# Conditioning weights loaded by halves of the channels, two blocks at once on four column groups, and a reordered rate stage, in a one-core decoder block

## The chip, the cores and the metric

The program runs on one core of a Trainium2 chip. The metric is the device time of one execution, in microseconds (us), taken as the median of several runs. Everything is computed in 32-bit floats; large products are made as three products of a high and a low part.

## The reference, cut to what matters

The kernel computes one decoder block for 1024 tokens of width 1024: adaLN conditioning, a mixing layer (RWKV-7 and latent attention side by side), and a mixture of 32 experts. The change touches how the block begins and how the rates of the RWKV branch are prepared.

```python
mod = jax.nn.silu(c) @ w_ada[l] + b_ada[l]            # (1, 6 * 1024)
sh_m, sc_m, gt_m, sh_f, sc_f, gt_f = jnp.split(mod, 6, axis=-1)
h = modulate(rmsnorm(x, g_norm_mix[l]), sh_m, sc_m)   # y * (1 + sc) + sh
z = h @ w_in[l]
...
w_log = -jax.nn.softplus(-(w0 + jnp.tanh(zw) @ w_decay_up)) - 0.5
decay = jnp.exp(-jnp.exp(w_log.astype(jnp.float32)))
a = jax.nn.sigmoid(a0 + za @ w_a_up)
kk = heads(zk * k_k).astype(jnp.float32)
kk = kk / jnp.maximum(jnp.sqrt(jnp.sum(kk * kk, axis=-1, keepdims=True)), 1e-12)
k = zk * (1 + (a - 1) * k_a)
```

So no product with `w_in` can be made before the shift and scale of its channels are known: 2048 columns of `w_ada` (8.4 MB), and the root mean square of each token row.

## The kernel before, in words

Each engine has its own hand-written stream of instructions; streams meet only at semaphores. SP issues nearly all transfers, in order, on one queue. The program is cut into blocks with a barrier between them; four stages matter here.

**Opening.** SP (line 421 on) asks for `c`, the whole table of constants (`cst`, 680 KB), seven of the eight 128-row tiles of `x` (512 KB each), biases and gains repeated over partitions, then eight pieces of `w_ada` of 1024 KB (one for each of eight interleaved groups of input channels `k`, all 2048 output columns; `Rows.load`, line 320). The eighth tile of `x` takes the place of the first in `xt` and is asked for only after that one has been transposed. ACT squares and sums each row tile (L543) and takes roots of four tiles at a time (L548); DVE scales the rows (L687); PE transposes them (L860) into three pairs of PSUM banks; ACT and DVE each copy one bank of a pair out (L552, L692) to `xn`, whose partitions are channels. In between, PE makes the conditioning products (`Rows.products`, L332): the vector silu(c), repeated over 32 columns as `crep`, is the stationary operand, and four blocks of 512 output columns go to the four column groups of the array, so that one PSUM bank holds shift and scale on four groups of 32 partitions. After the last piece DVE adds the bias (L339), makes (1 + scale) x gain (L709), PE turns the four blocks of rows to columns (L889), and DVE copies them to `mcol` (L712).

**Column tiles.** For each of eight channel groups `k`, ACT writes the high part of the modulated channels (`hh`, L572), DVE the exact value (L720) and the low part (`hl`, L351). PE then makes for `k` the products with the first two column tiles of `w_in` (24 matmuls of 512 columns, L355 to L357), whose own high and low parts are `wr_h` and `wr_l`. After all eight, PE goes on to the eight token tiles of the latent projections (`mla`, 24 matmuls of 416 columns each) and to the other column tiles, with the latent attention's preparation between them.

**Rates.** The next block, from 311 us: ACT squares the keys (L1022), PE sums them by head (L1099), ACT takes a root (L1025), DVE inverts it (L1054), PE spreads it back over the channels (`norms_back`, L1091). For each of four channel tiles PE makes two up-projections (decay and in-context rate, L1076), ACT two sigmoids and a scaled copy (L1029, L1032, L1037), DVE three products (L1058, L1063, L1064). The second row of conditioning (`rows2`: eight pieces of 1024 KB, L332) is loaded and multiplied in the same block; its buffer has room for six pieces.

**Scan.** The block after that starts with four prefix scans on DVE (L1451), their exponents (L1456, L1459) and exponentials on ACT (L1324 on), while POOL makes `rk` (L1245), clears `S` and builds four tiles `headrk` (L1293).

## Time and profile before

| | us |
|---|---|
| median of 3 runs (lowest, highest) | 1516.15 (1515.04, 1517.63) |
| the profiled execution's own time | 1512.1 |
| its span, first to last instruction | 1510.3 |
| PE busy in the span | 1381.2 (91%) |
| DVE busy | 761.9 (50%) |
| ACT busy | 492.7 (33%) |
| POOL busy | 317.5 (21%) |
| mean granted TensorE clock, share of 2.4 GHz | 0.961 |

A line of a timeline reads: start in the span, length, engine, line of the kernel, operation, output<-input, shapes, count; in brackets the time for which the engine stood idle before it and what ended that. A matmul of 32-bit floats shows as more than one record. PE is matmul time, PEld the loading of the stationary operand, which goes on beside it. "DMA packets" lines give what all queues moved in a stretch.

### The profile page before, as it was taken

Reading aid. Unit: us, or ns where it says so; the run is one execution under the profiler, and the core shown is the slowest. Engines: PE = TensorE matmul, PEld = TensorE weight load, DVE = VectorE, ACT = ScalarE, POOL = GpSimd, SP = SyncE. Lnnn points to the kernel's source line nnn. Section 1 sums busy time; section 2 is a strip of 40 time slices with the busy share of each in tenths; the row PEclk is TensorE's granted clock in tenths of the full one; section 3 lists DMA queues with packets and bytes.
Section 4 is the critical chain, followed back from the end, with each engine's and each line's share of the span. In section 5 each row is a group of like instructions: output and inputs, shape, how many; then the busy total and the mean of one; then the engine's idle time right before and its main releaser. Section 6 shows DMA issues by size and latency. Waiting matters only on the chain. (4 is left out here: it accounts for less than half of the span.)

```text
span 1510.3 us, 32868 instructions
## 1 busy us (share of the span) xinstructions
PE 1381.2 (91%) x14305; PEld 996.3 (66%) x14305; DVE 761.9 (50%) x1134; ACT 492.7 (33%) x891; POOL 317.5 (21%) x332
## 2 busy tenths in 40 slices
PE   4899999986999998899989999999996799999995
PEld 3587777745999998677767888787885333333332
DVE  3815676756677666544548455656455422111111
ACT  4433233263344443544445444313111111111110
POOL 0002121206556542011110000000000123333323
PEclk8999999997999999899999999999997699999998
DMA  9761322270000001750003113514227999999992
GB/s 372 278 187 51 91 75 66 75 268 2 4 4 4 4 11 41 207 202 15 15 27 141 56 56 112 195 53 161 84 84 274 358 354 392 382 403 380 394 370 59
DMA packets 74956, 238.20 MB, mean 158 GB/s; under 512 B 12216, under 2 KB 37304, under 8 KB 58048
## 3 DMA queue, kind: packets, MB, share of 16 engines
q1 hardware_dynamic: 63872, 219.31, 38.9%
q0 software_dynamic: 10944, 16.82, 4.6%
q8 instruction: 112, 1.84, 0.5%
q14 instruction: 28, 0.23, 0.0%
HBM read 207.74 MB, written 51.40 MB: 172 GB/s over the span
## 5 line engine op out<-in xcount | busy, mean ns | idle before, releaser
L3052 PE MATMUL ps<-gu,xT 128*32 128x512 f32 x1296 | 177.0, 605 | 4.9 <-DMA gu<-w_e_up 4.2
L3268 DVE TENSOR_TENSOR sg<-sg,ps 128x256 f32<-128x256 f32 x25 | 10.5, 421 | 205.4 <-ACT sg L3138 205.4
L3052 PEld LDWEIGHTS ps<-gu,xT 128*32 128x32 f32 x1296 | 46.8, 111 | 98.0 <-issue 94.4
L2939 POOL DMA_INDIRECT out<-YTM,home x48 | 75.2, 1566 | 168.2 <-DVE YTM L3277 160.9
L355 PE MATMUL ps<-hh,wr_h 128*128 128x512 f32 x224 | 93.5, 417 | 4.5 <-DVE hl L351 3.8
L357 PE MATMUL ps<-hh,wr_l 128*128 128x512 f32 x224 | 88.9, 397 | 0.0
L356 PE MATMUL ps<-hl,wr_h 128*128 128x512 f32 x224 | 88.9, 397 | 0.0
L3070 PE MATMUL ps<-dn,hidT 128*32 128x512 f32 x648 | 86.7, 592 | 0.5 <-ACT hidT L3142 0.5
L2119 DVE TENSOR_REDUCE nmax<-ps 128x1 f32<-128x896 f32 (+4 forms) x64 | 45.8, 752 | 71.4 <-PE ps L2017 70.9
L2957 POOL MEMSET xg<- 128x3072 f32 x1 | 2.7, 2658 | 366.1 <-PE ps L2444 366.1
L1287 POOL TENSOR_TENSOR off<-mats,cst 128x256 f32<-128x256 f32 x80 | 67.4, 861 | 48.0 <-PE ps L1709 47.7
L1502 DVE TENSOR_TENSOR inverses<-inverses,ps 128x512 f32<-128x512 f32 (+1 forms) x80 | 49.9, 630 | 50.8 <-PE ps L1725 50.4
L516 POOL TENSOR_TENSOR qk<-qk,g_row 128x768 f32<-128x768 f32 x16 | 37.9, 2390 | 173.3 <-DVE qk L792 173.3
L1725 PE MATMUL ps<-inverses,xx 64*64 64x64 f32 x1280 | 70.8, 218 | 0.0
L2012 PE MATMUL ps<-kT,qT 96*128 96x512 f32 (+3 forms) x160 | 64.8, 514 | 3.1 <-ACT causalr L2100 3.1
L3142 ACT ACTIVATE hidT<-ps 128x256 f32<-128x256 f32 x25 | 9.6, 384 | 166.5 <-PE ps L3039 166.5
L1722 PE MATMUL ps<-xx,inverses 64*64 64x64 f32 x1024 | 62.8, 220 | 0.2 <-issue 0.2
L1725 PEld LDWEIGHTS ps<-inverses,xx 64*64 64x64 f32 x1280 | 62.9, 135 | 0.1
L355 PE MATMUL ps<-hs,M 128*128 128x512 f32 x144 | 57.6, 400 | 1.6 <-DVE hs L351 1.6
L3052 PE MATMUL ps<-gu_last,xT 128*32 128x512 f32 x240 | 57.8, 594 | 0.0
L3070 PEld LDWEIGHTS ps<-dn,hidT 128*32 128x32 f32 x648 | 24.1, 110 | 50.3 <-issue 49.7
L356 PE MATMUL ps<-hs,M 128*128 128x512 f32 x144 | 56.1, 389 | 0.0
(440 smaller groups left out, 3433.3 us busy)
## 6 DMA issues: line engine op xcount, KB each, us to landing
gu<-w_e_gate SPq DMA_DIRECT2D x29, 1024.0 KB, 17.5
gu<-w_e_up SPq DMA_DIRECT2D x29, 1024.0 KB, 23.4
dn<-w_e_down SPq DMA_DIRECT2D x29, 1024.0 KB, 16.9
wbuf<-w_ada SPq DMA_DIRECT2D x16, 1024.0 KB, 12.8
wbuf<-w_ada SPq DMA_DIRECT2D x16, 512.0 KB, 4.6
wraws<-w_gates SPq DMA_DIRECT2D x16, 512.0 KB, 4.9
wr<-w_rwkv SPq DMA_DIRECT2D x14, 512.0 KB, 3.6
qk_cols<-YTM SPq DMA_DIRECT2D x8, 768.0 KB, 5.5
```

The lines of the kernel that those rows point to most:

```text
L355: nc.tensor.matmul(out, wt[0], mov[0], start=(k == 0), stop=False)
L356: nc.tensor.matmul(out, wt[0], mov[1], start=False, stop=False)
L357: return nc.tensor.matmul(out, wt[1], mov[0], start=False, stop=(k == kn - 1))
L1287: nc.gpsimd.tensor_tensor(off[:, g], mats[:, n % 2, 4 * g:4 * g + 4, 0], cst[:, a:a + CHUNK].unsqueeze(1).broadcast_to([P, 4, CHUNK]), ALU ...
L1502: nc.vector.tensor_tensor(now, now, add, ALU.add).then_inc(sm["t_ev"], 1)
L1722: nc.tensor.matmul(o[rows, 0:CHUNK], tt(j)[rows, hh, 1], xx[rows, hh], start=True, stop=True)
L1725: m = nc.tensor.matmul(o[rows, CHUNK:], xx[rows, hh], tt(j)[rows, hh, 1], start=True, stop=True)
L2012: nc.tensor.matmul(ps[:, 2 * (u % 2) + at // 512, at % 512:at % 512 + to - at], q, kT_[:, at - o * P:to - o * P], start=True, stop=True)
L2119: nc.vector.tensor_reduce(nmax[:, n:n + 1], score(u, i, o), AX.X, ALU.max, negate=True)\
L2939: pool.indirect_dma_start(out=out[0], out_offset=bass.IndirectOffsetOnAxis(ap=col.bitcast(u32), axis=0), in_=yo[:, buf], in_offset=None, b ...
L3052: last = nc.tensor.matmul(ps[part, GB[b]], xT[:, b, k, part], gu[expert(m, c_) % WB][:, :, k], start=(k == 0), stop=(k == KD - 1))
L3070: last = nc.tensor.matmul(ps[part, 6 + half], hidT[:, b, k, part], dn[expert(m, c_) % WB][:, k, half * 512:(half + 1) * 512], start=(k == ...
```

## The change

**Opening.** A new class `HalfRows` takes the place of `Rows` for the first 2048 conditioning columns. It loads sixteen pieces of 512 KB: for half `h` of the channels and input group `k`, 512 columns of shift and 512 of scale. First all eight pieces of half 0, then two column tiles of `w_in`, then half 1. One call of `products` takes two input groups `k` at once, each with two blocks, on the four column groups, and the bank then holds two partial sums of each, which are added after the transposition. Biases and gains come as 24 short rows that PE transposes to columns at the start. Only the 128-column identity of the constants is loaded early (behind two tiles of `x`), the rest after all transposes. The eighth tile of `x` has a place of its own (in `zm`), DVE squares tiles 1 and 3, and roots are taken two tiles at a time. PE begins with channel 0 when half 0 is modulated, with products of half 1 between channels 0, 1 and 2.

```diff
+            def load(self, sp, h, k):
+                src = w_ada_v[:, k, 0:2 * D].rearrange("p (a h n) -> p a h n", a=2, h=2)[:, :, h]
+                sp.dma_start(self.piece(h, k), src).then_inc(self.w_in[h][k // 2], 16)
+
+            def products(self, pe, h, pair):
+                if h == 0 and pair == 0:
+                    pe.wait_ge(self.rep_s, 1)
+                pe.wait_ge(self.w_in[h][pair], 32)
+                for i in range(2):
+                    for a in range(2):
+                        m = nc.tensor.matmul(ps[QUARTERS[2 * i + a], self.banks[h]], self.crep[:, 2 * pair + i],
+                                             self.piece(h, 2 * pair + i)[:, a], start=(pair == 0), stop=(pair == CT - 1))
+                m.then_inc(self.mm, 1)
+
+            def to_row(self, dve, h):
+                dve.wait_ge(self.mm, CT * (h + 1))
+                nc.vector.tensor_copy(self.row[:], ps[:, self.banks[h]]).then_inc(self.done, 1)
...
-                    sp.dma_start(cst[:], consts).then_inc(const_in, 16)
-                    for t in range(XT):
+                    for t in range(NT):
                         load_x(t)
+                        if t == 1:
+                            sp.dma_start(cst[:, 0:P], consts[:, 0:P]).then_inc(const_in, 16)
+                            rows0.load_bias(sp)
                     for k in range(KD):
-                        rows0.load(sp, k)
...
+                        rows0.load(sp, 0, k)
+                    for c_ in range(2):
+                        load_weights(c_)
+                    for k in range(KD):
+                        rows0.load(sp, 1, k)
                     sp.dma_start(wm[:], w_mla).then_inc(wm_in, 16)
+                    sp.wait_ge(tr, 2 * NT)
+                    sp.dma_start(cst[:, P:], consts[:, P:]).then_inc(const_in, 16)
...
+                    def columns(h):
+                        col = mcol[:, :, h]
+                        dve.wait_ge(mcol_mm, h + 2)
+                        sums_ = ps[:, 7].rearrange("p (j b a n) -> p b a j n", j=CT, b=2, a=2)[:, :, :, :, 0]
+                        nc.vector.tensor_tensor(col, sums_[:, 0], bg[:, 0:2, h], ALU.add).then_inc(mcol_s, 1)
+                        dve.wait_ge(mcol_s, 3 * h + 1)
+                        nc.vector.tensor_tensor(col, col, sums_[:, 1], ALU.add).then_inc(mcol_s, 1)
+                        dve.wait_ge(mcol_s, 3 * h + 2)
+                        nc.vector.tensor_tensor(col[:, 1], col[:, 1], bg[:, 2, h], ALU.mult).then_inc(mcol_s, 1)
...
+                    rows0.to_row(dve, 0)
+                    dve.wait_ge(bg_s, 2)
+                    columns(0)
+                    weights(0, 1)
...
+                    modulated(0)
+                    weights(1, 2)
+                    for k in range(1, CT):
+                        modulated(k)
+                    nc.vector.memset(zT[:, 0:2, 0:1], 0.0).then_inc(zero, 1)
+                    rows0.to_row(dve, 1)
+                    columns(1)
+                    dve.wait_ge(const_in, 32)
+                    dve.wait_ge(mcol_s, 6)
+                    for k in range(CT, KD):
+                        modulated(k)
```

**PE at the opening.** In the order of PE's instructions `cst,xt` and `cst,zm` are the transposes of `x`, `wbuf,crep` the conditioning products, `cst,arows` the turning of rows into columns. Before:

```order
L860 MATMUL ps<-cst,xt 128x128 x32
L332 MATMUL ps<-wbuf,crep 32x512 x8
L860 MATMUL ps<-cst,xt 128x128 x24
L332 MATMUL ps<-wbuf,crep 32x512 x16
L860 MATMUL ps<-cst,xt 128x128 x8
L332 MATMUL ps<-wbuf,crep 32x512 x8
L889 MATMUL ps<-cst,arows 128x128 x4
L355 MATMUL ps<-hh,wr_h 128x512
```

Now:

```order
L998 MATMUL ps<-cst,arows 128x24
L959 MATMUL ps<-cst,xt 128x128 x48
L380 MATMUL ps<-wbuf,crep 32x512 x4
L959 MATMUL ps<-cst,xt 128x128 x8
L380 MATMUL ps<-wbuf,crep 32x512 x4
L959 MATMUL ps<-cst,zm 128x128 x8
L380 MATMUL ps<-wbuf,crep 32x512 x8
L982 MATMUL ps<-cst,arows 128x128 x4
```

Sixteen of 32 conditioning products stand ahead of the first channel, the other sixteen between the first three channels (eight after channel 0, eight after channel 1).

**SP at the opening.** `xt` and `zm` are the tiles of `x`, `wbuf` the conditioning weights, `wr` and `wm` those of the first products. Now:

```order
L481 DMA ccol<-c 128x8
L477 DMA xt<-x 128x1024 x2
L485 DMA cst<-consts 128x128
L367 DMA arows<-b_ada 16x128
L368 DMA arows<-g_norm_mix 8x128
L477 DMA xt<-x 128x1024 x5
L477 DMA zm<-x 128x1024
L372 DMA wbuf<-w_ada 128x2x512 x8
L480 DMA wr<-w_rwkv 128x1024 x2
L372 DMA wbuf<-w_ada 128x2x512 x8
L493 DMA wm<-w_mla 128x3328
L495 DMA cst<-consts 128x1232
```

Before, the constants stood second, and all eight pieces of 1024 KB were asked for ahead of the rest.

**Rates.** The selection matrix `sel` and the first two of the eight pieces of `rows2` are loaded in the block before (the buffer now has five places, one of them laid so that it is free early); up-projections are made rate by rate, not half by half of the tokens, so that the decay's sigmoid can start after two products; the first products of `rows2` stand between the sums by head.

```diff
-                        for n in range(2):
-                            for j, (w, src, done) in enumerate(((wup[0:64], Z(WA)[0:64], dec),
-                                                                (wup[64:128], Z(WA)[64:128], a_done))):
-                                if c_ and n == 0:
-                                    pe.wait_ge(done, c_)
+                        for j, (w, src, done) in enumerate(((wup[0:64], Z(WA)[0:64], dec),
+                                                            (wup[64:128], Z(WA)[64:128], a_done))):
+                            if c_:
+                                pe.wait_ge(done, c_)
+                            for n in range(2):
                                 m = nc.tensor.matmul(ps[:, 6 * j + n], w[:, c_ * P:(c_ + 1) * P],
                                                      src[:, n * 512:(n + 1) * 512], start=True, stop=True)
-                                if n:
-                                    m.then_inc(up_mm, 1)
+                            m.then_inc(up_mm, 1)
```

**PE in the block of the rates.** `zT,YTM` are up-projections, `sq,norm_sel` sums by head, `rn,norm_sel` norms spread back, `wbuf,crep` products of `rows2`. Before:

```order
L1076 MATMUL ps<-zT,YTM 128x512 x4
L1099 MATMUL ps<-sq,norm_sel 32x256 x16
L1091 MATMUL ps<-rn,norm_sel 128x256 x4
L332 MATMUL ps<-wbuf,crep 32x512 x4
L1076 MATMUL ps<-zT,YTM 128x512 x4
L1091 MATMUL ps<-rn,norm_sel 128x256 x4
L332 MATMUL ps<-wbuf,crep 32x512 x4
```

Now:

```order
L1190 MATMUL ps<-zT,YTM 128x512 x4
L1211 MATMUL ps<-sq,norm_sel 32x256 x8
L339 MATMUL ps<-wbuf,crep 32x512 x4
L1211 MATMUL ps<-sq,norm_sel 32x256 x8
L339 MATMUL ps<-wbuf,crep 32x512 x8
L1204 MATMUL ps<-rn,norm_sel 128x256 x4
L339 MATMUL ps<-wbuf,crep 32x512 x4
L1190 MATMUL ps<-zT,YTM 128x512 x4
L1204 MATMUL ps<-rn,norm_sel 128x256 x4
L1190 MATMUL ps<-zT,YTM 128x512 x4
```

Four of the eight products of `rows2` now come before the second up-projection, and none between the later channel tiles.

**Scan.** POOL waits for the four scans of the first period before it starts, and the four `headrk` tiles are built by DVE behind its first exponents.

```diff
+                    wait("cum", 0, CT)
                     prepare(0)
                     nc.gpsimd.memset(S[:], 0.0).then_inc(init, 1)
-                    for c_ in range(CT):
-                        nc.gpsimd.tensor_scalar(headrk[:, c_], C("heads"), PC("r_k", c_), None, ALU.mult)\
-                          .then_inc(init, 1)
...
+                    for c_ in range(CT):
+                        nc.vector.tensor_scalar(headrk[:, c_], C("heads"), PC("r_k", c_), None, ALU.mult)\
+                          .then_inc(init, 1)
```

## Rows read from the trace of the kernel before

**Rows 1.** The page's first line: span of the profiled execution.
```profile
span 1510.3 us, 32868 instructions
```
**Rows 2.** DMA answer, stretches 7 to 12, 36 to 41 and 41 to 48 us.
```profile
DMA packets 571, 2.08 MB, mean 415 GB/s; under 512 B 64, under 2 KB 64, under 8 KB 571
...
DMA packets 260, 2.16 MB, mean 432 GB/s; under 512 B 31, under 2 KB 31, under 8 KB 31
...
DMA packets 1206, 2.21 MB, mean 316 GB/s; under 512 B 128, under 2 KB 940, under 8 KB 1132
```
**Rows 3.** Timeline of the opening, 6 to 32 us: row tiles of x.
```profile
6.95 1.06 ACT L543 ACTIVATE tmp<-xt 128x1024 f32<-128x1024 f32 x1 [4.21 <-DMA xt<-x]
...
13.71 2.74 DVE L687 TENSOR_SCALAR xt<-xt,rs 128x1024 f32<-128x1024 f32 x4
...
16.51 0.33 SPq L428 DMA_DIRECT2D xt<-x  x1
16.52 0.69 DVE L692 COPY xn_late<-ps 128x512 f32<-128x512 f32 x1
...
27.90 1.06 ACT L543 ACTIVATE tmp<-xt 128x1024 f32<-128x1024 f32 x1 [7.21 <-DMA xt<-x]
...
30.55 5.38 PE L860 MATMUL ps<-cst,xt 128*128 128x128 f32 x24 [7.81 <-DVE xt L687]
```
**Rows 4.** Timeline, 35 to 51 us: from the last conditioning weights to the first product.
```profile
35.86 3.82 PE L332 MATMUL ps<-wbuf,crep 128*32 128x512 f32 x32
...
41.79 0.16 PEld L332 LDWEIGHTS ps<-wbuf,crep 128*32 128x32 f32 x8 [1.00 <-DMA wbuf<-w_ada]
...
44.16 0.68 DVE L339 TENSOR_TENSOR arows<-arows,ps 128x512 f32<-128x512 f32 x1
...
45.62 0.66 PE L889 MATMUL ps<-cst,arows 128*128 128x128 f32 x4 [2.77 <-DVE arows L709]
46.32 0.17 DVE L712 COPY mcol<-ps 128x16 f32<-128x16 f32 x1 [0.75 <-PE ps L889]
...
46.53 1.24 ACT L572 ACTIVATE hh<-YTM,mcol 128x1024 fp32r<-128x1024 f32 x1 [3.74 <-DVE mcol L712]
...
47.90 0.81 DVE L720 TENSOR_SCALAR YTM<-YTM,mcol 128x1024 f32<-128x1024 f32 x1 [1.41 <-ACT hh L572]
...
48.75 1.23 DVE L351 TENSOR_TENSOR hl<-YTM,hh 128x1024 fp32r<-128x1024 f32 x1
...
50.12 0.77 PE L355 MATMUL ps<-hh,wr_h 128*128 128x512 f32 x1 [3.84 <-DVE hl L351]
```
**Rows 5.** Windows: length, busy PE, PEld, DVE, ACT, POOL, clock, DMA share, GB/s.
```profile
50.00:53.00 3.00, 2.88 (x7) 2.33 (x8) 2.93 (x4) 3.00 (x4) 0.00 (x0) 0.50 1.06 370
53.00:76.00 23.00, 23.00 (x102) 18.84 (x101) 21.25 (x34) 7.63 (x6) 1.39 (x1) 0.99 0.58 225
```
**Rows 6.** Timeline at 74 us: the first latent product.
```profile
74.06 0.35 PE L355 MATMUL ps<-wm_h,hh 128*128 128x416 f32 x1
```
**Rows 7.** The loads of column tiles (L431), 512 KB each: least, median, most.
```profile
DMA to landing us min/median/max: 3.2/3.6/17.1
```
**Rows 8.** Timeline of the rates, 312 to 343 us.
```profile
312.54 1.99 PE L1076 MATMUL ps<-zT,YTM 64*128 64x512 f32 x8 [1.74 <-DMA norm_sel<-norm_sel]
...
319.50 2.45 PE L1091 MATMUL ps<-rn,norm_sel 32*128 32x256 f32 x8 [3.10 <-DVE rn L1054]
...
323.74 3.29 PE L1076 MATMUL ps<-zT,YTM 64*128 64x512 f32 x8
...
327.07 1.11 ACT L1029 ACTIVATE lw<-ps,pc 128x1024 f32<-128x1024 f32 x1 [5.13 <-PE ps L1076]
...
337.00 4.50 PE L332 MATMUL ps<-wbuf,crep 128*32 128x512 f32 x40
```
**Rows 9.** Timeline of the scan's start, 342 to 358 us.
```profile
342.88 2.53 DVE L1451 TENSOR_TENSOR_SCAN cum<-cst,lw 128x128 f32<-128x128 f32 x4 [0.55 <-PEq L1004]
...
355.74 1.37 DVE L1451 TENSOR_TENSOR_SCAN cum<-cst,lw 128x128 f32<-128x128 f32 x4 [2.18 <-PE ps L1629]
```

More of the change, by code:

```diff
@@ L208, in build @@
         mod_out = ctx.enter_context(nc.semaphore("mod_out"))
[L209 removed]
+        up_in, sel_in = (ctx.enter_context(nc.semaphore(n)) for n in ("up_in", "sel_in"))
+        first_rows = [ctx.enter_context(nc.semaphore(f"first_rows{i}")) for i in range(2)]
         y_out4 = ctx.enter_context(nc.semaphore("y_out4"))
@@ L309, in __init__, with place @@
                 self.b_in, self.mm, self.done = sems(st, f"ab_in{col}", f"amm{col}", f"adone{col}")
-                self.w_in = slots(st, f"aw_in{col}", self.room)
+                self.w_in = list(first) + slots(st, f"aw_in{col}", self.room - len(first))
+                self.order = order or list(range(self.room))
+            def place(self, i):
+                return self.wbuf[:, self.order[i % self.room]]
             def cols(self, j):
@@ L900, in _ @@
                                 m.then_inc(z_mm, 1)
+                    pe.wait_ge(const_in, 16)
+                    pe.wait_ge(rows0.b_in, 32)
+                    nc.tensor.transpose(ps[:, 7, 0:24], small0[0:24], C("ident")[0:24, 0:24]).then_inc(mcol_mm, 1)
+                    for t in range(NT):
+                        row_transposes(t)
+                        if t >= NT - 3:
+                            for pair in range(t - NT + 3, t - NT + 4 if t < NT - 1 else CT):
+                                rows0.products(pe, 0, pair)
+                    row_columns(0)
+                    channel(0)
+                    for pair in range(2):
+                        rows0.products(pe, 1, pair)
+                    channel(1)
+                    for pair in range(2, CT):
+                        rows0.products(pe, 1, pair)
+                    channel(2)
+                    row_columns(1)
+                    for k in range(3, KD):
+                        channel(k)
                     def half_column(c_, n):
@@ L1006, in _ @@
                 def _(sp):
-                    for k in range(CT):
+                    for k in range(2, CT):
                         rows2.load(sp, k)
```

242 lines of the change are left out of this document (138 added, 104 removed).

## The prediction

> **What bounds the kernel now.** I read the page first, then windows and the timeline of the two stages that the change touches. PE is busy for 91% of the span, so over most of the kernel a change elsewhere is worth nothing. The exceptions are stretches in which PE has no work yet, and there each microsecond counts, because the later stages start on events of the earlier ones: whatever comes off the front shifts all that follows. The span is 1510.3 us [rows 1], the profiled execution's own time 1512.1, the median 1516.15; I make the sum against the execution and lay the difference on the median, which is 4.05 above it.
>
> **The opening** is bound by transfers. The last piece of the conditioning weights lands at 41.79 and the first real product starts at 50.12 [rows 4]. Up to then the queue has moved 0.70 MB of constants, 4.19 of `x`, 8.39 of `w_ada`, 1.05 of `wr` and some biases, 14.7 MB in about 39.5 us, without a pause. The rate depends on the packet: 415 GB/s with packets of 4 KB, 432 with 8 KB and more, 316 where most are of 1 KB [rows 2]. A second delay hides in it: the eighth tile of `x` is asked for at 16.51, behind four pieces of 1 MB, and its squares start at 27.90, with ACT idle for 7.21 us, and PE for 7.81 until its transposes at 30.55 [rows 3]. From the last piece to the first product runs a chain with no slack: product, bias, gain, turning, copy, high part, exact value, low part, 41.79 to 50.12, so 8.3 us [rows 4]. After that PE is full: 3 us at a clock of 0.50 (the 1.2 GHz level, after PE had been nearly idle), then 0.99 (2.4 GHz) with 23.00 of 23 us busy [rows 5]. The first latent product starts at 74.06 [rows 6], 23.9 us after the first channel.
>
> **The rates**, from 311 to 342 us, are a chain over PE, ACT and DVE. PE waits 1.74 for `norm_sel`, later 3.10 for the inverse norms, and ACT waits 5.13 for the second up-projection [rows 8]. PE ends the block with five products, 337.00 to 341.5.
>
> **Part 1, up to the first product: 15.3 us less.** When does half 0 land? `x` starts at about 2.2 us and takes 4.19/0.415 = 10.1. Half 0 is 4.19 MB in packets of 2 KB. No row shows that size; between 316 and 415 GB/s [rows 2] I take 365, since packets of 4 KB run close to those of 8 and only those of 1 KB fall off: 11.5 us. With 1.5 us for the landing itself (0.70 MB of constants and a first tile of 0.52 take 2.9 at that rate from 2.2, and its squares start at 6.95 [rows 3]), half 0 has landed at 25.3, the pair of `wr` at 27.8, and half 1 (another 11.5) at 39.3.
>
> Row preparation is no longer hidden and decides. DVE starts on it at about 8 (identity and short biases stand behind two tiles of `x`). It has two squarings (two-input, as L351, 1.23 [rows 4]; I take 1.3), eight scalings (2.74 for four [rows 3]) and eight copies of 0.69 [rows 3], and four round trips for roots at about 0.9: 2.6 + 5.5 + 5.5 + 3.6 = 17.2, so 25.2. Laid out tile by tile with the waits for PE (5.38 for three tiles [rows 3], so 1.8 a tile, and the last tile is scaled at 24.2), the last copy ends at 27.7. The last two pairs of products follow PE's last transposes: a pair is as much work as one piece before, 3.82/4 = 0.95 [rows 4], so about 29.0. Then the copy to a row 0.69, turning 0.66, three small operations at 0.2 in place of one of 0.17 (the wide gain operation goes), high part 1.2, exact value 0.81, low part 1.23, handovers 0.5 [rows 4]: 5.7. The weights' low part lies beside the high part on ACT. First product at 34.8 in place of 50.12. Bounds: 32, where half 0's landing and the same chain alone count; 38.5, where each of the last four tiles costs another microsecond of waiting between ACT, DVE and PE.
>
> **Part 2, channels: 5.1 us given back.** What came before the channels partly moves into them: four pairs of products for half 1, 3.8 (3.5 without the last one's tail), the second turning, 0.5. PE reaches it at 34.8 + 13.7 = 48.5. DVE and ACT then need three small operations, high part, exact value and low part, 3.9, under channel 3, which takes 23.0/8 = 2.9 [rows 5]: PE waits about 1.1. Behind DVE's wait for the constants stand all four late channels, but these land at 39.3 + 1.70/0.43 + 0.63/0.4 = 45, and the wait is reached at 49. Half 1 is needed at 34.8 + 8.7 = 43.5, 4 us after it lands. Channels take 29.0 in place of 23.9. Bounds: 3.8 with no wait, 8 if half 1 or the constants are late. The latent stage thus starts 10.2 us earlier. SP's queue: rows4, gains and the spill of `h` stand behind the same bytes as before and end at about 66; DVE asks for them at 61, but its work there is wanted by PE only some 20 us later. I cost that at nothing.
>
> **Part 3, rates: 5.0 us less.** The first up-projection no longer waits 1.74, but the root behind it is held by ACT's squares and its table load, so that is worth 0. After 319.50 eight products of `rows2` lay on PE's path (three between, five at the end, 4.50/5 = 0.9 each), now five: 2.7. The 3.10 us gap before 319.50 is filled with two products, so the clock should stay up, and the first spreading (2.45) and the second up-projection (3.29) each get back up to half: 2.9 at most, of which I take 2.3. The order rate by rate starts ACT's sigmoid half a projection (1.0) earlier, but PE's own 3.3 a round then decides. Bounds 2.7 and 6.5. The two early pieces cost the block before nothing: PE is full there and the queue is not.
>
> **Part 4, scan: 1.2 us less.** The first four scans take 2.53 beside POOL, the next four 1.37 without [rows 9]. POOL now waits for them, and 2.53 - 1.37 = 1.16. Four small operations move to DVE, hidden while ACT makes the exponentials; if not, they cost 0.7. Bounds 0 and 2.5.
>
> **Sum.** 15.3 - 5.1 + 5.0 + 1.2 = 16.4 us off: 1512.1 - 16.4 = 1495.7 for such an execution, and **1499.7** for the median. That the products share four column groups adds nothing: four were in use before, and as many matmuls remain.
>
> A rule that speaks against the change: the halves make sixteen transfers of 512 KB of eight of 1024. What the trace shows: eight transfers of 512 KB behind each other ran at 415 GB/s [rows 2], 1.26 us each, while one of that size alone takes 3.2 from issue to landing [rows 7], about 2 more. The Trainium skill (DMA: Bandwidth & Descriptors, Bandwidth) says to batch transfers to 1 MiB or more to get three quarters of the peak, and gives 341 GB/s for a single one of 1 MB. By that rule the fixed part would be paid for each half piece, and the sum would become the last rival's below; by the row the pieces overlap, and the sum stands.
>
> **Rivals.**
> - **Row preparation is slower than laid out** (0.17). For: DVE, ACT and PE hand each tile round, and ACT has its squares between copies. Against: bare work sums to 25. First product at 39: 1499.7 + 4.2 = 1503.9.
> - **Only the front gains** (0.07): the rates stay bound by PE at the low clock or by ACT. 1499.7 + 5.0 = 1504.7.
> - **It all comes out better** (0.11): first product at 32, no wait inside the channels, 6.5 from the rates: 1499.7 - 2.8 - 1.1 - 1.5 = 1494.3.
> - **The shift is swallowed later** (0.03), at a transfer that does not start on an event: no change, 1516. Against: I found none; SP's waits at the experts are on PE and DVE.
> - **Slower: transfers of half size pay their fixed part one by one** (0.02). At 2 us each [rows 2, 7], sixteen land half 1 31 us later, at 70. From its landing to the latent stage run one pair 0.95, the chain of 5.2 and four channels, 11.2: 17.4 us. The stage would start at 87.7 instead of 74.06, and with 6.2 from the other parts the time is 1516.15 + 13.6 - 6.2 = 1523.5. It decides from a landing at 63 on. Against stands the row of 415 GB/s.
>
> **How the numbers follow.** The forecast has 0.60. Its own bounds, not all at one end, give 1495 to 1504. The range takes in the first three rivals as well: 1494 to 1507, which leaves out less than 2 in 10. Faster by over 0.2% (3 us, about what a measurement of this kernel can tell from no change): 0.95. Within: 0.03. Slower: 0.02.
>
> **What would show it.** The first product of 128x512 with `wr_h` at 34.8 (32 to 38.5); DVE's last copy at 27.7, after half 0's landing at 25.3; the first latent product at 63.8 with a gap of PE near 1 us behind channel 3; the block of the rates 5 us shorter, with ACT's second sigmoid waiting well under 5 us; the first four scans near 1.4. I am wrong if half 1 or the constants hold DVE, if the clock stays at 1.2 GHz beyond some 3 us of channel 0, or if the rates end within 2 us of before.

## The result, and the profile after

| | before | changed |
|---|---|---|
| median (lowest, highest), us | 1516.89 (1515.04, 1518.90) | 1503.57 (1501.70, 1504.10) |
| runs | 4 | 4 |
| profiled execution's own time | 1512.1 | 1503.23 |
| its span | 1510.3 | 1501.4 |
| PE busy in the span | 1381.2 (91%) | 1380.9 (92%) |
| mean granted clock | 0.961 | 0.965 |

The ratio is 0.9919, 95% interval 0.9900 to 0.9938: 13.3 us faster between the medians, where 16.4 were forecast. The interval runs from 9.4 to 15.2 us, so the forecast saving lies just outside it. The two profiled executions differ by only 8.9: single executions scatter by several us, and the last experiments measure by how much.

The opening of the changed kernel, as a timeline (start, length, engine, line, operation), 19 to 35 us. These rows answer to [rows 3] and [rows 4]:

```profile
24.43 0.69 DVE L760 COPY xn_late<-ps 128x512 f32<-128x512 f32 x1 [1.33 <-PE ps L959]
...
25.88 1.07 PE L380 MATMUL ps<-wbuf,crep 128*32 128x512 f32 x8 [0.49 <-DMA wbuf<-w_ada]
27.01 0.69 DVE L386 COPY arows<-ps 128x512 f32<-128x512 f32 x1 [1.89 <-PE ps L380]
27.14 1.06 ACT L389 ACTIVATE wr_h<-wr 128x1024 fp32r<-128x1024 f32 x1 [2.55 <-DMA wr<-w_rwkv]
...
28.92 0.16 DVE L777 TENSOR_TENSOR mcol<-mcol,arows 128x4 f32<-128x4 f32 x1
...
29.31 1.06 ACT L389 ACTIVATE wr_h<-wr 128x1024 fp32r<-128x1024 f32 x1 [1.11 <-DMA wr<-w_rwkv]
30.27 4.62 ACT L634 ACTIVATE hh<-YTM,mcol 128x1024 fp32r<-128x1024 f32 x4
...
31.63 0.81 DVE L782 TENSOR_SCALAR YTM<-YTM,mcol 128x1024 f32<-128x1024 f32 x1 [1.42 <-ACT hh L634]
32.48 1.23 DVE L392 TENSOR_TENSOR hl<-YTM,hh 128x1024 fp32r<-128x1024 f32 x1
...
33.76 0.79 PE L396 MATMUL ps<-hh,wr_h 128*128 128x512 f32 x1 [5.34 <-DVE hl L392]
```

Three things are to be seen. The last copy of the rows (L760) ends at 25.12, and only then, at 25.88, do the last two pieces of half 0 let PE go on: the landing of half 0 ends last, not the row preparation. The columns are ready at 29.08, but ACT waits 1.11 us for the second weights (`wr`, which stand behind half 0 on the queue), makes their high part first and gets to `hh` at 30.27. The first product starts at 33.76.

The same timeline from 44 to 53 us, the turning of half 1 and the gap behind the fourth channel. The kernel before has nothing in this place:

```profile
44.87 0.69 DVE L386 COPY arows<-ps 128x512 f32<-128x512 f32 x1 [4.06 <-PE ps L380]
...
47.62 0.60 PE L982 MATMUL ps<-cst,arows 128*128 128x128 f32 x4
48.26 0.17 DVE L773 TENSOR_TENSOR mcol<-ps,arows 128x8 f32<-128x8 f32 x1 [2.70 <-PE ps L982]
...
52.36 0.50 PE L396 MATMUL ps<-hh,wr_h 128*128 128x512 f32 x1 [1.34 <-DVE hl L392]
```

The rows of half 1 are out of PSUM at 45.56 and wait two microseconds for PE, which turns them only behind the third channel, at 47.62. From there to the low part runs the same chain as for half 0, and PE stands for 1.34.

Windows of the changed kernel (length, busy time of PE, PEld, DVE, ACT, POOL, clock, DMA share, GB/s) answer to [rows 5]:

```profile
33.80:36.70 2.90, 2.90 (x7) 2.32 (x8) 2.87 (x3) 1.09 (x1) 0.00 (x0) 0.51 1.04 386
36.70:50.00 13.30, 13.30 (x75) 8.17 (x75) 5.23 (x10) 1.14 (x1) 0.00 (x0) 1.00 1.05 350
50.00:63.60 13.60, 12.26 (x53) 9.65 (x52) 11.43 (x9) 7.41 (x6) 1.60 (x1) 1.00 1.04 403
```

And the DMA answer for 15.0 to 25.5 us, while half 0 lands, answers to [rows 2]:

```profile
DMA packets 2036, 4.09 MB, mean 390 GB/s; under 512 B 126, under 2 KB 126, under 8 KB 2036
```

The low clock takes 2.9 us of the first channel, about as before the change, and packets of 2 KB run at 390 GB/s.

The rates, which answer to [rows 8]:

```profile
307.91 1.06 PE L339 MATMUL ps<-wbuf,crep 128*32 128x512 f32 x8 [1.24 <-DMA wbuf<-w_ada]
...
308.98 1.47 PE L1204 MATMUL ps<-rn,norm_sel 32*128 32x256 f32 x8
...
311.05 1.06 PE L339 MATMUL ps<-wbuf,crep 128*32 128x512 f32 x8 [0.60 <-DMA wbuf<-w_ada]
...
312.05 2.00 PE L1190 MATMUL ps<-zT,YTM 64*128 64x512 f32 x8
...
314.07 1.11 ACT L1143 ACTIVATE lw<-ps,pc 128x1024 f32<-128x1024 f32 x1 [2.55 <-PE ps L1190]
...
322.88 3.64 PE L339 MATMUL ps<-wbuf,crep 128*32 128x512 f32 x32
323.43 1.28 DVE L1172 SCALAR_TENSOR_TENSOR kk<-zT,pc,ps 128x1024 f32<-128x1024 f32 x1
...
326.14 1.22 DVE L1178 TENSOR_TENSOR aa<-aa,kk 128x1024 f32<-128x1024 f32 x1
```

The spreading (2.45 before) and the second up-projection (3.29 before) run at the full clock. ACT waits 2.55 us for the second up-projection, where it waited 5.13 before. The last four products of `rows2` end at 326.5, while DVE is still at its three products: no longer PE but DVE ends the block. And two products of `rows2` wait for their weights, 1.24 and 0.60 us. Only the second of these waits holds the up-projection: during the first PE had to wait for the inverse norms anyway, which DVE has ready at 308.92.

The scan's start, which answers to [rows 9]:

```profile
328.51 1.37 DVE L1572 TENSOR_TENSOR_SCAN cum<-cst,lw 128x128 f32<-128x128 f32 x4 [0.55 <-PEq L1118]
329.92 0.69 DVE L1577 TENSOR_TENSOR ex<-cum,lw 128x512 f32<-128x512 f32 x1
329.96 1.77 POOL L1368 TENSOR_TENSOR rk<-zT 128x512 f32<-128x512 f32 x1 [28.58 <-DVE cum L1572]
330.53 1.75 DVE L1580 TENSOR_TENSOR ex<-cum 128x512 f32<-128x512 f32 x1
...
332.32 1.06 ACT L1445 ACTIVATE ex<-ex 128x1024 f32<-128x1024 f32 x1 [2.56 <-DVE ex L1580]
...
338.31 0.68 DVE L1605 TENSOR_TENSOR zT<-zT,ps 128x512 f32<-128x512 f32 x1
...
339.14 1.09 PE L1753 MATMUL ps<-cst,ce 128*128 128x128 f32 x4 [3.01 <-DVE zT L1605]
```

The scans take 1.37, as forecast, but POOL now runs beside the second exponent, which takes 1.75; the kernel before makes it in 0.68 (there it is L1459, started at 346.18). The last two lines are the end of the chain to the first pair: DVE's last multiplication (L1605), and behind it PE's transposes of `ce` and `ex`, here at the lower clock (1.09 and 1.06). In the kernel before, with its scan's start at 342.88, the same multiplication stood here:

```profile
352.89 0.67 DVE L1484 TENSOR_TENSOR zT<-zT,ps 128x512 f32<-128x512 f32 x1
```

So it starts 10.01 us behind the scan's start before, and 9.80 after the change.

Starts in the span of each execution, read off the timelines (the two first columns are the two kernels of the table above, "again" is a second execution of each):

| | before | changed | before again | changed again |
|---|---|---|---|---|
| first product | 50.1 | 33.8 | 50.1 | 33.5 |
| first latent product | 74.1 | 63.6 | 73.9 | 63.5 |
| rates | 311.3 | 300.9 | 311.2 | 300.7 |
| scan | 342.9 | 328.5 | 342.8 | 328.8 |
| first pair of the scan | 356.4 | 341.9 | 356.3 | 341.3 |
| attention | 621.8 | 610.2 | 623.3 | 611.7 |
| experts | 1190.4 | 1180.0 | 1193.3 | 1180.5 |
| end | 1510.3 | 1501.4 | 1516.1 | 1501.0 |

### The profile page after: what moved, and what is told of

Same layout as the page of the kernel before. It is cut to its first block and busy times, and to the rows that moved or that the text cites. A ratio compares the mean times of both kernels' runs of the same rounds, so it can differ in the third digit from the quotient of the medians.

```text
span 1501.4 us, 32904 instructions
## 1 busy us (share of the span) xinstructions
PE 1380.9 (92%) x14310; PEld 996.1 (66%) x14310; DVE 762.7 (51%) x1153; ACT 490.3 (33%) x890; POOL 314.7 (21%) x328
## 5 line engine op out<-in xcount | busy, mean ns | idle before, releaser
L396 PE MATMUL ps<-hs,M 128*128 128x512 f32 x144 | 57.6, 400 | 1.6 <-DVE hs L392 1.6
L396 PEld LDWEIGHTS ps<-hh,wr_h 128*128 128x128 f32 x224 | 42.6, 190 | 20.9 <-DVE hl L392 7.4
## 6 DMA issues: line engine op xcount, KB each, us to landing
wbuf<-w_ada SPq DMA_DIRECT2D x8, 1024.0 KB, 10.2
```

Source lines behind the costliest of these rows:

```text
L396: nc.tensor.matmul(out, wt[0], mov[0], start=(k == 0), stop=False)
```

## The experiments

The theories were these. A: what the profile shows up to the scan's first pair is the whole effect, its parts add, and the rest is scatter. B: part of it is given back later, or one part carries all. The times of one group come from the same chip, with the kernel before run beside them. "Ratio" is against that kernel.

### One part alone, smaller transfers, POOL one step later

**Only the opening.** The changed kernel with the rates, their early loads and the scan as before. The core of what is undone:

```diff
-                            if c_:
-                                pe.wait_ge(done, c_)
-                            for n in range(2):
+                        for n in range(2):
...
+                                if c_ and n == 0:
+                                    pe.wait_ge(done, c_)
...
-                    wait("cum", 0, CT)
                     prepare(0)
```

> Only the new opening; block of the rates and scan as before. Theory A (the parts add and nothing is given back later): first latent product at 63.6 as with the whole change, start of the rates 10.4 us earlier than before, and the whole 9 to 11 us below the kernel before (1506 to 1508). Theory B (a shift of the front is partly given back in later stages, 1.2 us in the scan, 1.8 at the attention's start, 1.5 to 3 after it): same start of the rates, but only 5 to 7 us below before.

Measured: median 1504.81 (6 runs; before 1514.5, 17 runs), ratio 0.9928, interval 0.9911 to 0.9946, so 9.7 us between the medians, and 10.9 by the ratio (8.2 to 13.5). That is what A forecast; B's 5 to 7 lie below the interval. First product 33.7, first latent product 64.8, rates at 302.0: 9.2 us earlier than before, where 10.4 were expected. What is missing is the clock: with the same opening it stayed at its lower level for 5.6 us from the first product here, for 2.9 in the changed kernel's profile.

**Only the rates.** The kernel before, its opening and scan untouched, with the early loads and the new order:

```diff
+                            sp.dma_start(wbuf2[:, 0], row_piece(2 * D, 0, 512)).then_inc(first_rows[0], 16)
...
+                    norm_sums(0)
+                    norm_sums(1)
+                    rows2.products(pe, 0)
+                    norm_sums(2)
+                    norm_sums(3)
```

> Only the new block of the rates with its early loads; opening and scan as before. Theory A: the block is 4.0 us shorter (31.6 before, 27.6), the whole 3.5 to 4.5 us below before. Theory B: the block is as much shorter, the whole less than 2.5 us below before. If the block saves less than 3 us, the new order works only together with the new opening.

Measured: median 1513.23 (12 runs), ratio 0.9993, interval 0.9979 to 1.0008. In its profile the block takes 27.6 us (311.6 to 339.2) instead of 31.6, so 4.0 less, and the first pair comes 4.4 us earlier. The time shows 1.3 of it, at most 3.2 by the interval, which is B's number. A part of the reason may be below, where the block is seen to vary: in three of nine executions it saves clearly less than 4.

**Pieces of half the size.** 32 transfers of 256 KB instead of 16 of 512:

```diff
-                src = w_ada_v[:, k, 0:2 * D].rearrange("p (a h n) -> p a h n", a=2, h=2)[:, :, h]
-                sp.dma_start(self.piece(h, k), src).then_inc(self.w_in[h][k // 2], 16)
+                for a in range(2):
+                    c0 = a * D + h * 512
+                    sp.dma_start(self.piece(h, k)[:, a], w_ada_v[:, k, c0:c0 + 512]).then_inc(self.w_in[h][k // 2], 16)
```

> The changed kernel with 32 transfers of 256 KB in place of 16 of 512 KB for the conditioning weights, packets of 2 KB as now. If fixed parts of transfers overlap behind each other: half 0 lands within 0.5 us of now and the time stays within 1 us of the changed kernel (about 1503.5). If each transfer pays 2 us one by one: eight more for half 0, landing 16 us later, and the time is 15 us above the changed kernel or more. A third, weaker form, 0.1 to 0.3 us a transfer: 1 to 3 us above.

Measured: 1504.32 (6 runs), ratio 0.9932, interval 0.9918 to 0.9945; first product 33.1, first latent product 63.6. The DMA answer for its 15 to 25 us:

```profile
DMA packets 2087, 3.90 MB, mean 390 GB/s; under 512 B 231, under 2 KB 231, under 8 KB 2087
```

The same 390 GB/s as with 512 KB. Transfers behind each other on the queue do not pay their fixed part one by one, at half the size either. The slower rival is refuted. By the Trainium skill (DMA: Bandwidth & Descriptors, Bandwidth) transfers should be batched to 1 MiB or more; here the trace differs: transfers stand behind each other on the queue, and in both kernels their packets take 105% of the 16 engines' time in this stretch.

**POOL behind the exponents.** The changed kernel waits for the scans alone, and the second exponent is slowed. So let POOL wait for both exponents:

```diff
-                    wait("cum", 0, CT)
+                    wait("pre", 0, 2)
```

> The changed kernel, but POOL waits for the first period's two exponent operations on DVE too, not for the scans alone. If POOL's product beside it is what stretches the second exponent operation from 0.68 to 1.75: it takes about 0.7, ACT's first exponential starts 1.0 us earlier after the block's start (3.86 now), and the first pair products come about 1 us earlier in the block; whole 0.5 to 1.5 us below the changed kernel. If another cause stretches it (the operation's broadcast, say), it stays at 1.75 and nothing moves.

Measured: 1503.42 (6 runs), ratio 0.9924, interval 0.9907 to 0.9941. From the scan's start to its first pair 14.7 us, where the changed kernel has 13.4: worse. Its timeline:

```profile
330.91 0.68 DVE L1580 TENSOR_TENSOR ex<-cum 128x512 f32<-128x512 f32 x1
331.51 3.25 DVE L1678 TENSOR_SCALAR zT<-cst,pc 128x128 f32<-128x128 f32 x4
331.63 1.06 ACT L1445 ACTIVATE ex<-ex 128x1024 f32<-128x1024 f32 x1 [1.49 <-DVE ex L1580]
331.67 1.28 POOL L1368 TENSOR_TENSOR rk<-zT 128x512 f32<-128x512 f32 x1 [30.38 <-DVE ex L1580]
```

The exponent is at 0.68 and the exponentials start earlier, as meant. But POOL now runs beside the four small multiplications, which take 3.25 instead of 0.86, and DVE gets to the factors only at 334.68. The collision was moved, not removed, and the factors themselves (L1586) then take 1.68 instead of 0.69. The Trainium skill (SBUF — State Buffer, Terms) says that VectorE and GpSimd arbitrate for one pair of ports, and that the loser is held for the other's whole instruction. The rows agree in the size: 1.07 us more for VectorE beside an operation of GpSimd that takes 1.28 to 1.77.

### Four single moves in the changed kernel

The changed kernel was not timed in this group. Its ratios in the other groups (0.9919 twice, intervals from 0.9900 to 0.9938) overlap with all four intervals below, so the total times do not tell what one move is worth; the traces have to.

**POOL behind all of it.** POOL waits for the four `headrk` tiles as well:

```diff
-                    wait("cum", 0, CT)
+                    pool.wait_ge(init, CT)
                     prepare(0)
```

> GpSimd's first multiplication waits for VectorE's four small multiplications as well, so that it runs beside no VectorE operation ahead of the exponentials. Theory A (GpSimd and VectorE slow each other when they run side by side: an operation of 0.68 us took 1.75, four that took 0.86 together took 3.25): all three groups of VectorE at their short times (0.69, 0.68, 0.86), the exponentials about 1.0 us earlier, first pair of the scan 12.3 us after the scan's first operation instead of 13.4 (changed kernel) and 14.7 (GpSimd behind the exponents only). Theory B (the bonus products, which need GpSimd's result, are on the path): first pair 13.4 or later.

Measured: 12.3 us from the scan's start (332.0) to its first pair (344.3). The timeline has all three groups short:

```profile
333.37 0.69 DVE L1577 TENSOR_TENSOR ex<-cum,lw 128x512 f32<-128x512 f32 x1
333.98 0.68 DVE L1580 TENSOR_TENSOR ex<-cum 128x512 f32<-128x512 f32 x1
334.58 0.87 DVE L1678 TENSOR_SCALAR zT<-cst,pc 128x128 f32<-128x128 f32 x4
...
335.53 1.28 POOL L1368 TENSOR_TENSOR rk<-zT 128x512 f32<-128x512 f32 x1 [34.38 <-DVE zT L1678]
...
335.78 1.57 DVE L1586 SCALAR_TENSOR_TENSOR factors<-kk,ex 128x512 f32<-128x512 f32 x1 [0.34 <-ACT ex L1445]
...
341.59 0.67 DVE L1605 TENSOR_TENSOR zT<-zT,ps 128x512 f32<-128x512 f32 x1
...
342.41 0.63 PE L1753 MATMUL ps<-cst,ce 128*128 128x128 f32 x4 [2.10 <-DVE zT L1605]
```

The number is A's, 12.3 against 13.4, but A's reason explains only a small part of it. The exponentials do start 1.1 us earlier. But now POOL's multiplication runs beside DVE's first factors, which take 1.57 instead of 0.69, and DVE's last multiplication (L1605) starts 9.6 us behind the scan's start, where it was 9.8 in the changed kernel: 0.2 gained. The other 0.8 come behind it, where PE's two transposes ran at the full clock (0.63 and 0.60 instead of 1.09 and 1.06). The changed kernel itself, in its second profile, has these transposes at the full clock too and reaches the first pair in 12.5 us, with no edit at all. So the late wait is shown to be worth 0.2 us. Both executions with it had the full clock there, against one of seven with the wait of the change; whether it helps the clock is open.

The whole: 1502.05 (6 runs; before 1516.75, 11 runs), ratio 0.9903, interval 0.9886 to 0.9920. The block of the rates, untouched here, took 31.4 us in this execution:

```profile
308.44 1.07 PE L339 MATMUL ps<-wbuf,crep 128*32 128x512 f32 x8 [1.44 <-DMA wbuf<-w_ada]
309.44 1.99 PE L1204 MATMUL ps<-rn,norm_sel 32*128 32x256 f32 x8
...
312.15 1.93 PE L339 MATMUL ps<-wbuf,crep 128*32 128x512 f32 x8 [0.72 <-DMA wbuf<-w_ada]
...
314.01 3.48 PE L1190 MATMUL ps<-zT,YTM 64*128 64x512 f32 x8
```

The third and fourth products of `rows2` wait for their weights, the clock falls to its lower level during the spreading between them (1.99 instead of 1.47, then 1.93 instead of 1.06 and 3.48 instead of 2.00), and nearly all of the forecast gain of the rates is gone: 31.6 was the time before. The length of these waits doesn't decide the clock: the run with all squares on ACT (below) has longer ones, 1.82 and 1.37 us, and keeps the full clock; its block takes 28.9.

**The fourth product of `rows2` behind both up-projections.** It moves from ahead of the second up-projection to the end:

```diff
-                    rows2.products(pe, 3)
...
-                    for k in range(CT, KD):
+                    for k in range(CT - 1, KD):
```

> The fourth of the eight row products of the rates' block is issued behind both up-projections instead of ahead of the second. Theory A (the row products between the up-projections wait for landings of 0.6 to 1.2 us and hold the second up-projection): block of the rates 26.4 instead of 27.7 us, whole -1 us if later stages pass it on. Theory B (the last exponents wait for something else, the product is only moved): block 27.7 us, whole 0.

Measured: 1500.94 (6 runs), ratio 0.9894, interval 0.9877 to 0.9912. The second up-projection starts 9.6 us behind the block's start instead of 11.2, but in this execution it ran at the lower clock:

```profile
310.56 3.60 PE L1190 MATMUL ps<-zT,YTM 64*128 64x512 f32 x8
```

so that the block took 27.9 and not 26.4 (its wait for the fourth product was gone, so the clock can fall without that one too). With the wait gone and the clock up it takes 26.2, in the kernel of the next group.

**Turning half 1 inside the third channel.**

```diff
                         for c_ in range(2):
+                            if k == 2 and c_ == 1:
+                                row_columns(1)
...
                     channel(2)
-                    row_columns(1)
```

> The second half's rows are turned into columns in the middle of the third channel's products instead of after them. Theory A (the wait of ScalarE for the second half's columns, 2.7 us of VectorE's idle time before L773 in the changed kernel, then the exact product and the low part, is what TensorE waits for behind the fourth channel): the turned columns come some 2 us earlier, the gap behind the fourth channel's products goes, first latent product 62.4 instead of 63.6, whole -1.2 us. Theory B (rows are not done in time at the new place, TensorE waits there instead): first latent product at 63.6 or later.

Measured: the turning starts at 46.58 instead of 47.62, and the gap of 1.34 us behind the fourth channel is gone. First latent product 62.6, which is 1.1 earlier. Theory A. The whole 1501.50 (6 runs), ratio 0.9894, interval 0.9876 to 0.9913; the block of the rates took 30.0 here, with waits of 1.48 and 1.07 for the same landings and the lower clock after the second.

**`hh` of the first channel ahead of the second weights' high part.**

```diff
-                    for c_ in range(2):
-                        weights(c_, 16)
+                    weights(0, 16)
                     act.wait_ge(xn_a, NT)
                     act.wait_ge(xn_d, NT)
                     for k in range(KD):
+                        if k == 1:
+                            weights(1, 16)
```

> ScalarE makes the high half of the first modulated channel before the high part of the second weights (it began at 30.27 us in the changed kernel, held by the weights' landing and 1.06 us of work, though the columns it reads were ready at 29.1). Theory A (that queue position costs the front about 1.2 us): the first modulated channel begins at 29.1, the first product at 32.6 instead of 33.8, the first latent product at 62.4 instead of 63.6, whole -1.2 us. Theory B (the second weights' high part then comes too late for the first channel's second column tile): first product 32.6, but the products of the second column tile wait and the first latent product stays at 63.6, whole 0.

Measured: first product 32.5 (1.3 earlier), first latent product 63.6 as in the changed kernel; whole 1502.37 (6 runs), ratio 0.9909, interval 0.9891 to 0.9928. B's number, but not B's reason: the windows show PE without a gap, and at the lower clock for 5.5 us instead of 2.9:

```profile
32.50:35.50 3.00, 3.00 (x7) 2.42 (x8) 2.96 (x4) 2.08 (x2) 0.00 (x0) 0.50 1.05 388
35.50:38.00 2.50, 2.50 (x10) 1.46 (x13) 2.47 (x4) 0.00 (x0) 0.00 (x0) 0.50 1.08 403
38.00:50.00 12.00, 12.00 (x69) 7.34 (x70) 2.70 (x7) 1.22 (x2) 0.00 (x0) 1.00 1.05 345
```

2.6 us more at half the clock are 1.3 us of full-speed work: what the earlier start had won. The earlier start need not be the reason. With the first product at 33.7 the opening-only kernel had 5.6 us at the lower clock, and the kernel with all squares on ACT (33.1) had 5.0. So the move removes ACT's wait, and what it is worth behind that isn't settled by one profile.

### What ended last in the opening, the three useful moves together, and both kernels again

**All squares on ACT.** This asks whether the row preparation has room. The tiles that DVE squares go back to ACT:

```diff
-            ON_DVE = (1, 3)
+            ON_DVE = ()
```

> All eight tiles' squares on ScalarE, none on VectorE. Theory A (in the changed kernel the landing of the first half's last piece, 0.5 us of TensorE's wait ahead of L380 at 25.88, and not the preparation of the rows ends last, with 0.8 us of room behind the last copy at 25.1): up to 0.8 us of delay is hidden and the rest shows; two more squares of 1.25 us on ScalarE in the stretch that ends with the last tiles move the last copy from 24.4 to about 27, first product 35.5 instead of 33.8, rates start 302.5. Theory B (ScalarE has room, the copies come by TensorE's turns): first product stays at 33.8.

Measured: first product 33.1; whole 1502.73 (6 runs; before 1515.62, 11 runs), ratio 0.9919, interval 0.9901 to 0.9938. PE waits longer for the last pieces, not shorter:

```profile
26.13 1.06 PE L380 MATMUL ps<-wbuf,crep 128*32 128x512 f32 x8 [1.14 <-DMA wbuf<-w_ada]
```

The half of A that says that the landing ends last holds, the half that says that the copies would come late does not: the rows are ready even earlier without DVE's squares (last copy done at 24.7, not 25.1). That the first product comes 0.6 earlier here is the second pair of weights: ACT waits 0.23 us for them instead of 1.11. This landing varies from execution to execution (0.21 to 1.73 of waiting). So does that of half 0: PE waits 0.3 to 1.1 us for its last pieces in seven of eleven profiles, and not at all in four; in those four ACT waits 1.0 to 1.7 us for the second weights. Either way a landing is the last to end.

**Three moves together**: the late wait of POOL, the fourth product moved, the early turning.

> Three single moves together in the changed kernel: the second half's rows turned in the middle of the third channel, the fourth row product of the rates' block behind both up-projections, GpSimd's first multiplication of the scan behind VectorE's four small ones. Theory A (each sits on the path and they add): first latent product 62.6 (as with the first alone), block of the rates 27.7 or shorter whatever the landings, 12.3 us from the scan's first operation to its first pair, together 1.3 + 0.5 to 3.5 + 1.0 us, the whole at 1500 us, ratio to the kernel before 0.989. Theory B (what they save is waited for again behind the scan): whole at 1502 to 1503.5 as each alone, ratio 0.991.

Measured: 1498.39 (4 runs; before 1515.62, 11 runs), ratio 0.9886, interval 0.9868 to 0.9905. The changed kernel beside it, on the same chip, has 1502.58. First latent product 63.2, block of the rates 26.2 (300.4 to 326.6), scan's start to first pair 12.3:

```profile
307.38 1.06 PE L339 MATMUL ps<-wbuf,crep 128*32 128x512 f32 x8 [1.15 <-DMA wbuf<-w_ada]
...
309.94 2.00 PE L1191 MATMUL ps<-zT,YTM 64*128 64x512 f32 x8
```

This is the fastest version of the study, 4.2 us below the changed kernel by the medians; the intervals against the kernel before overlap, so the size of that step is known roughly only. In the profile the first pair of the scan comes 2.9 and 2.3 us earlier than in the two profiles of the changed kernel, and the scan's share is again the clock of the transposes. The early turning brought just 0.4 here, as the lower clock lasted longer after 36.7:

```profile
36.70:50.00 13.30, 13.30 (x72) 8.08 (x71) 5.49 (x11) 1.62 (x2) 0.00 (x0) 0.93 1.06 357
```

**The kernel before again.** A copy, for a second profile.

> The kernel before, profiled a second time, to see how far its stages move by themselves. Theory A (the 2 to 4 us that the changed kernel seems to give back between the scan's first pair and the end are scatter of single executions: the kernel before was profiled 4.8 us under its median): opening, block of the rates and scan's start within 0.2 us of the first profile (50.1, 311.3, 342.9), from the scan's first pair to its last 206 to 207.5 us instead of 205.6, end later than 1510.3. Theory B (the later stages are slower because of the change): 205.6 and 1510.3 again within 0.5 us.

Measured: 1517.97 for its run, span 1516.1. Up to the scan's first pair each stage starts within 0.2 us of the first profile. Behind it the second execution is 5.9 us longer: 0.3 in the scan (A had expected 0.4 or more there), 1.3 between the scan's last pair and attention, 1.5 at the products behind attention, 2.8 in the experts.

**The changed kernel again.**

> The changed kernel again, profiled and timed beside the others. Theory A (scatter of single executions in the later stages and in the landings of the rates' row weights): first product 33 to 34, first latent product 63.5, block of the rates 27.7 to 31.4 with the start of the second up-projection 11.2 to 13.4 us behind the block's start; whole 1503 us, ratio 0.991. Theory B: the block takes 27.7 again and the stages behind it the same as the first time within 0.5 us each.

Measured: 1502.58 (6 runs), ratio 0.9919, interval 0.9904 to 0.9934, the same ratio as the first time. First product 33.5, block of the rates 28.1, second up-projection 11.6 us behind the block's start, end 1501.0. Scan's start to first pair 12.5, with the transposes at the full clock, where the first profile has 13.4.

The two executions of the kernel before differ by 5.8 us, and the second pair of profiles has the changed kernel 15.1 us ahead. From the scan's first pair to the end the 14 profiled executions of this study, none of which changes anything there, took 1153.9 to 1159.9 us, and the shortest of all is the first profile of the kernel before. So a pair of profiles can't show whether part of the gain is given back later. A give-back of about 1 us isn't excluded: the stretch from the scan's last pair to attention took 60.6 to 61.9 us in the eleven profiles with the new opening, and 59.6, 59.9 and 60.9 in the three without it.

## Why the prediction was right, and where its steps were off

**The first product: 34.8 forecast, 33.8 measured (33.0 to 33.8 in the kernels with the changed opening and ACT's order).** The path was the one named (half 0, turning, modulation, first product), but the step "Row preparation is no longer hidden and decides" failed. The last copy was to end at 27.7 and ended at 25.12, at the sum of the bare work (25.2) and without the 2.5 us laid on for waits between engines. The landing decides instead. It was forecast well, by two errors that largely cancelled: packets of 2 KB ran at 390 GB/s, not 365 (10.7 us for half 0, not 11.5), while what lies ahead of half 0 ended some 1.4 us later than worked out (an estimate: 25.88 less 10.7 and the 1.5 for the landing is 13.7, against 12.3). The 415 GB/s taken for all of `x` is the rate of the stretch from 7 to 12 us, about four tiles; from 2 to 7 us the changed kernel moved 1.52 MB at 304 GB/s. The last pair of products starts at 25.88 where 25.3 was the landing. The rival that row preparation is slower lost its ground by the run with all squares on ACT. In the chain behind the last products 5.7 us were forecast and 6.8 measured (27.01 to 33.76): the second weights and their high part were taken to be hidden and held `hh` by 1.2 (by 0.3 in the second profile, where they landed earlier). So the number came out within 1.0 partly by luck: the products ended 2.1 us earlier than forecast, and the chain took 1.1 longer.

**Channels: 5.1 given back forecast, 5.9 measured** (63.6 - 33.8 = 29.8 against 23.9). The gap behind channel 3 was 1.34, forecast 1.1, and it goes when the turning moves. The latent stage came 10.4 us earlier, forecast 10.2.

**Rates: 5.0 forecast, 4.0 measured in the first profile, 0.3 to 4.0 over the nine profiles with this order.** The clock's part was right in seven of the nine: 2.45 became 1.47 and 3.29 became 2.00, together 2.3, as taken. Two steps failed. "PE's own 3.3 a round then decides": DVE and ACT decide, the three products of DVE start at 310.50, 315.49, 319.77 and 323.43, so rounds of 5.0 (with the 0.60 of waiting in it), 4.3 and 3.7. And no term stood for the landing of the third and fourth pieces of `rows2`, which now lie ahead of the second up-projection. They cost 0.60 us ahead of the fourth product in the first profile and 0.50 to 1.37 in the others. In two of the nine the clock fell as well, and in one of these nearly the whole gain was gone; as longer waits passed without a fall, what makes it fall there stays open. With the fourth product moved behind, the block took 26.2, 5.4 less than before, in the profile that kept the clock and 27.9 in the one that did not. Nor is the fast clock all the reordering's merit: with the rates as before and only the new opening, the block took 30.1 instead of 31.6, because in that execution the spreading of the norms ran at the full clock (1.46 instead of 2.45) without any change to it.

**Scan: 1.2 forecast, 0.2 measured in the first profile, 1.0 in the second.** 2.53 did become 1.37. The step that failed is the unsaid one that POOL's multiplication would be in nobody's way once it was late: it met DVE's second exponent, 0.68 became 1.75. On DVE's path, up to its last multiplication ahead of the first pair, the change won 0.2 in both profiles; the 0.8 between them are PE's transposes at one clock or the other. With POOL behind all of DVE's first operations another 0.2 came off that path and no more, since POOL then met the factors (0.69 became 1.57). Wherever POOL's multiplication was put, it met an operation of DVE, so the forecast 1.2 never came out on that path.

**The sum**: 16.4 forecast; 14.6 at the scan's first pair (15.0 in the second pair of profiles), 13.3 and 13.0 between medians. Up to the first pair the rates and the scan are 1.0 short each, and the opening is 0.2 better than forecast. Behind it another 1 to 2 us are missing. That may be the rates and the clock in the executions that weren't profiled, or a give-back ahead of attention; it stays open. The opening alone carries 9.7 of it by time; of the 4.0 that the rates show in a profile the time of that kernel alone confirms 1.3 (at most 3.2). Varying landings and the clock can lower the mean below 4.0; whether they explain all of it isn't settled, since timed executions leave no trace.

## What to carry to other kernels

When work is moved ahead of a waiting chain, its own inputs move ahead too: look at when they land, and leave at the back whatever isn't certain to be there. An engine's delayed start moves a collision and need not remove it: a start of GpSimd later by two operations of VectorE cost 1.3 us, and later by six it won 0.2 on VectorE's path. Follow the path to its end before crediting an edit with the time that came off: here 0.8 of 1.0 us were the clock of two groups of transposes. And before explaining what a profile seems to lose in stages that weren't changed, profile the kernel before a second time: here its first execution was the shortest of fourteen in those stages.

## What the runs showed of the hardware that was not expected

- VectorE and GpSimd slow each other when both work: 0.68 to 1.75 us for one 128x512 operation, 0.86 to 3.25 for four of 128x128 (GpSimd's own multiplication took 1.77 beside the first and 1.28 beside the second), 0.69 to 1.57 for the factors.
- How long TensorE stays at the lower clock varies with the same opening: from a first product at 33.8 the granted clock stayed at 0.50 for 2.9 us, in another kernel from one at 33.7 for 5.6, and from one at 32.5 for 5.5. That is worth up to 1.4 us, more than single moves in the opening win.
- In the block of the rates the granted clock stayed up through waits of 1.82 and 1.37 us in one execution and fell behind one of 1.44 in another.
- Transfers of 256 KB and of 512 KB behind each other, both in packets of 2 KB, ran at the same 390 GB/s.
